# Moving sixteen modulation sums of VectorE from the stick-breaking attention to the retention, with attention steps 1.3 to a row

## The reference

```
mod = silu(c) @ w_ada + b_ada                 # 1024 -> 6144: shift1, scale1, gate1, shift2, scale2, gate2
hmix = rmsnorm(x) * (1 + scale1) + shift1
proj = hmix @ w_in                            # attention q, k, v; retention q, k, v, g; branch gates
o_sb  = stick_breaking_attention(16 heads of 64)
o_ret = silu(r_g) * head_rmsnorm(retention(rotary(q), rotary(k), v))   # 4 heads, q and k 256 wide, v 512
x = x + gate1 * ((g_sb * (o_sb @ w_proj_sb) + g_ret * (o_ret @ w_proj_ret)) @ w_out)
x = x + gate2 * ffn(rmsnorm(x) * (1 + scale2) + shift2)
```

## Time and profile before

| | |
|---|---|
| median of 3 runs | 2096.8 us (2093.87 to 2098.34) |
| the profiled execution | 2099.07 us, its span 2097.2 us |
| mean granted TensorE clock | 0.965 |
| attention with q, k, v and gate | about 61 to 330 us of the span |
| product with w_proj_sb | about 350 to 395 us |
| retention | about 395 to 850 us |

### The profile page before, as it was taken

The page is one execution under the profiler, slowest core; times in us unless marked ns, Lnnn a source line. Parts: engine busy times, 40 slices in busy tenths (PEclk is TensorE's granted clock), DMA queues, the critical chain, the costliest instruction groups (busy, mean ns, idle before and its releaser), DMA issues.

```text
span 2097.2 us, 21914 instructions
## 1 busy us (share of the span) xinstructions
PE 1955.8 (93%) x8805; PEld 1524.1 (73%) x8805; DVE 893.5 (43%) x1486; ACT 716.1 (34%) x1032; POOL 499.7 (24%) x270
## 2 busy tenths in 40 slices
PE   7989989999999999969599999998898889999998
PEld 6666667877777777857488888865775578888886
DVE  6677776203031313342133333468535554433433
ACT  5645464123332323332122223423236432222223
POOL 4322224444444434400000000132235411000000
PEclk9999999999999999979799999998998989999999
DMA  9323324421313123212522322421121122322321
GB/s 305 118 81 101 101 75 155 162 81 61 101 61 101 61 81 120 82 59 46 126 83 81 118 91 65 111 81 60 50 72 61 41 71 81 100 101 81 101 91 50
DMA packets 183771, 192.21 MB, mean 92 GB/s; under 512 B 10034, under 2 KB 167000, under 8 KB 183544
## 3 DMA queue, kind: packets, MB, share of 16 engines
q1 hardware_dynamic: 181816, 183.46, 27.6%
q10 hardware_dynamic: 1424, 5.00, 0.7%
q0 software_dynamic: 432, 2.36, 0.3%
HBM read 186.09 MB, written 4.72 MB: 91 GB/s over the span
## 4 chain that ended last, share of the span: by engine, by line
PE 45%; DVE 6%; DMA 2%; issue 2%; ACT 1%; POOL 0%; SPq 0%; DVEq 0%; ACTq 0%; POOLq 0%
PE bank L1402 12%; PE bank L1403 11%; PE bank L1405 11%; DMA stg<-in_w_ffn_in 2%; PE bank L1424 2%; PE bank L1423 2%; PE bank L1422 2%; DVE SW L2019 1%; DVE small L2017 1%; PE bank L1640 1%; PE bank L1662 1%; PE bank L1577 0%; DVE wl L1715 0%; PE bank L1528 0%; PE bank L1432 0%
## 5 line engine op out<-in xcount | busy, mean ns | idle before, releaser
L2541 POOL TENSOR_TENSOR wl<-stg,wh 128x1024 fp32r<-128x1024 f32 x150 | 362.1, 2415 | 1065.5 <-ACT wh L2199 1065.4
L1402 PE MATMUL bank<-hH,wh 128*128 128x512 f32 x1296 | 543.6, 419 | 47.6 <-DVE wl L1715 39.9
L1403 PE MATMUL bank<-hL,wh 128*128 128x512 f32 x1296 | 522.1, 403 | 0.0
L1405 PE MATMUL bank<-hH,wl 128*128 128x512 f32 x1296 | 521.4, 402 | 0.0
L2199 ACT ACTIVATE wh<-stg 128x1024 fp32r<-128x1024 f32 (+2 forms) x292 | 298.3, 1023 | 327.5 <-PE bank L1405 211.8
L1402 PEld LDWEIGHTS bank<-hH,wh 128*128 128x128 f32 x1296 | 249.8, 193 | 134.3 <-issue 79.0
L1405 PEld LDWEIGHTS bank<-hH,wl 128*128 128x128 f32 x1296 | 249.5, 192 | 61.0
L1403 PEld LDWEIGHTS bank<-hL,wh 128*128 128x128 f32 x1296 | 250.6, 193 | 51.7 <-issue 0.7
L1715 DVE TENSOR_TENSOR wl<-stg,wh 128x1024 fp32r<-128x1024 f32 (+2 forms) x142 | 168.4, 1188 | 270.1 <-ACT wh L2199 269.5
L1402 PE MATMUL bank<-h2H,wh 128*128 128x512 f32 x352 | 141.3, 402 | 0.0
L1405 PE MATMUL bank<-h2H,wl 128*128 128x512 f32 x352 | 140.7, 400 | 0.0
(11 more groups left out here) (321 smaller groups left out, 2763.2 us busy)
## 6 DMA issues: line engine op xcount, KB each, us to landing
stg<-in_w_in SPq DMA_DIRECT2D x54, 1024.0 KB, 5.1
stg<-in_w_ffn_in SPq DMA_DIRECT2D x22, 1024.0 KB, 5.1
stg<-in_w_ada SPq DMA_DIRECT2D x16, 1024.0 KB, 5.3
stg<-in_w_ffn_gate SPq DMA_DIRECT2D x11, 1024.0 KB, 5.1
stg<-in_w_ffn_up SPq DMA_DIRECT2D x11, 1024.0 KB, 5.1
stg<-in_w_ffn_down SPq DMA_DIRECT2D x10, 1024.0 KB, 5.0
stg<-in_w_ada SPq DMA_DIRECT2D x16, 512.0 KB, 6.5
stg<-in_w_proj_ret SPq DMA_DIRECT2D x8, 1024.0 KB, 4.9
```

Source lines behind the costliest of these rows:

```text
L1402: T.matmul(ps, wh, xh, start=j["first"] and k == 0, stop=False)
L1403: T.matmul(ps, wh, xl, start=False, stop=False)
L1405: t = T.matmul(ps, wl, xh, start=False, stop=j["stop"] and last)
L2541: G.tensor_tensor(lo, src, hi, ALU.subtract).then_inc(s["w_lo_pool"], 1)
```

## The change

The sixteen blocks leave the attention, the branch gate and the w_proj_sb product. One is placed behind every pair of jobs of q, k, v and g in the retention until all are used: six at head 0, six at head 1, four at head 2. `adasum` is no longer put off: it stands directly behind the pair of jobs, and takes its bank from "G" and no longer from "O". The sum lies in one buffer of its own, ADA, of 128x256, and a block's first DVE instruction waits for the `adasum` of the block before (it was two before). The attention's rate goes from 1 to 1.3 in the q, k, v jobs and in the branch gate's.

```diff
         def fn(n):
             for _ in p.jobs[n]["steps"]:
                 pass
-
-            def sums():
-                take("O", ("mod", a), 0)
-                emit("adasum", a)
-                give(("mod", a))
-            p.later.append([0, sums])
+            take("G", ("mod", a), 0)
+            emit("adasum", a)
+            give(("mod", a))
         return fn
...
-    left = list(range(8, 24))
     for p2 in range(1, 4):
         for kind, b0 in (("sbq", 0), ("sbk", 1024), ("sbv", 2048)):
             both(b0 + p2 * 256, kind, [(2 * p2,), (2 * p2 + 1,)], "w_in", "h1", after=v_after if kind == "sbv" else None)
-            ada(left.pop(0))
-        stage(1)
+        stage(1.3)
...
         both(O_BR + f2 * 256, "gate_sb", [(2 * f2,), (2 * f2 + 1,)], "w_in", "h1", after=tables_again)
-        if left:
-            ada(left.pop(0))
-    stage(1.0)
+    stage(1.3)
     do(p.finish)
     for f2 in range(4):
         both(f2 * 256, "proj_sb", [(2 * f2,), (2 * f2 + 1,)], "w_proj_sb", "os")
-        if left:
-            ada(left.pop(0))
     stage()
...
+    left = list(range(8, 24))
+
+    def more_ada():
+        if left:
+            ada(left.pop(0))
+
     def qk_jobs(hh):
         for what, o0 in (("q", O_RQ), ("k", O_RK)):
             b = p.block("w_in", o0 + hh * 256)
             for half in range(2):
                 p.job(b, half, rot_job(what, hh, half), x="h1")
+            more_ada()
...
(the same line at the end of each turn of the loops in v_jobs and g_jobs)
...
+        ADA = sb("ADA", [P, 256])
...
-            return TMP[7][:, 256 * (n % 2):256 * (n % 2) + 256]
+            return TMP[7][:, 256 * (n % 2):256 * (n % 2) + 256] if n < 8 else ADA[:, :]
...
-                        ve.wait_ge("pe_ada", n - 1)
+                        ve.wait_ge("pe_ada", n - 1 if n < 8 else n)
```

## The result

The changed kernel takes 2110.9 us (median of 4 runs, 2106.6 to 2111.5); the kernel before took 2096.6 beside it (4 runs, 2093.9 to 2098.3). The ratio is 1.0055, 95% interval 1.0039 to 1.0071: slower, clear of the noise, and 2.6 us from the forecast of 2108.3. The profiled execution is the fastest of the four, 2106.57 us with a span of 2104.8; that of before, 2099.07 us, lies above its four. The two profiled executions therefore differ by 7.5 us where the medians differ by 14.3; no trace tells where the other runs spent their 4 us more.

The account below looks back on a forecast made before the run. PE was taken to bound the retention alone, DVE to cost only in the attention. Terms: -2.7 - 1.7 - 1.4 + 1.5 + 10.7 + 5.1 = +11.5 us, giving 2110.6 profiled, 2108.3 as median; range 2086 to 2119.

Parts of the forecast that it names:

- Which stage is bound by what: DVE work costs something in the attention only; the retention is bound by PE alone, so waits there are paid in full.
- The bank: Retention: `adasum` takes a "G" bank, so PE waits 1.8 us for the rotation's third instruction, six times: +10.7 us.
- The clock: Stalls bring the lower granted clock, 1.7 us lost each: -1.7 us in the attention, +5.1 us in the retention.
- one less, -1.7 us: Attention: of six stretches at the lower clock one goes, -1.7 us (-8.5 to +1.7).
- Modulation out of the attention: Attention: removal saves 3.8 us a pair, rate 1.3 takes 2.1 back; waits become 17 us, -2.7 us (-13.6 to +5).
- The bare chain: Attention: at rate 1.3 PE stands 1.2 us in every pair from the attention's own DVE chain, without modulation.
- Cover and load: Attention, a pair: rate 1.3 costs 2.1 us of time PE covers for DVE; removed modulation instructions free 3.8 us.
- the rival by which the port hands its waits over: Attention: chain DVE instructions wait for the shared port instead; pairs +5 us, clock unchanged, 2117.7 us; chance 0.15.
- The start: Attention's start: up to one more softplus piece stands ahead of ACT's copy of q, +1.5 us.
- Bank 7: Attention: PE's wait at `adasum` behind the single bank 7 goes, -1.4 us.
- DVE's sums done 5 us before PE asks: Retention: DVE has room and finishes a block's sums some 5 us before PE asks; taken as 0 us (0 to +3).
- 16 us lower without it: Retention: were `adasum` left in bank 7, there would be no rotation wait and the sum would be 16 us lower.

Follow-up runs that it names:

- e1: The changed kernel with the bank of `adasum` taken from the two of "Z" instead of the three of "G": 2104.3 us, ratio to the kernel before 1.0023.
- e4: The changed kernel with the second and third instruction of the rotation (L1811, L1812) exchanged: 2107.7 us, ratio to the kernel before 1.0046.
- e11: e10 with the bank of `adasum` taken from "G", as in the change: 2100.4 us, ratio to the kernel before 1.0021.
- e3: The changed kernel with both attention rates back at 1, modulation still in the retention, `adasum` on "G": 2102.3 us, ratio to the kernel before 1.0021.
- e2: The kernel before with both attention rates at 1.3, the modulation left where it was: 2109.7 us, ratio to the kernel before 1.0054.
- e5: e1 with both attention rates back at 1: 2100.1 us, ratio to the kernel before 1.0014.
- e9: e1 with the retention's q, k, v and g jobs prepared three jobs ahead instead of two while modulation blocks are left: 2104.5 us, ratio to before 1.0037.
- e10: e9 with the attention's rates at 1: 2095.8 us, ratio to the kernel before 0.9992.
- e12: e10 with `adasum` put off by one job and two halves of a sum buffer: 2088.1 us, ratio to the kernel before 0.9961.
- e14: e12 with the attention's rates at 1.3: 2092.5 us, ratio to the kernel before 0.9982.
- e15: e12 with the attention's rates at 0.9: 2072.8 us, ratio to the kernel before 0.9887.
- e13: e12 with two jobs of lead instead of three: 2095.8 us, ratio to the kernel before 0.9998.

## Why the prediction was right

- *Which stage is bound by what*: right. The retention paid for its waits in full.
- *The bank*: right, and shown by e1, e4 and e11. 12.7 us in six waits against 10.7; 10.2 of it are the wait as reckoned, six times 1.70 us against 1.8, and the rest is DVE late twice, which I had named without a price. No run has the bank of "G" with `adasum` put off, so what the bank costs by itself there stays open.
- *The clock*: the retention's 6.8 us against 5.1. In the attention the step "one less, -1.7 us" was wrong in size: five of six stretches went, 8.5 us. The stalls before were up to 2.6 us; in the changed kernel none at L1464 is over 1.82. But stalls of 1.82 us were followed by a stretch before, and the one of 1.82 in the changed kernel isn't, so why five went stays open.
- *Modulation out of the attention*: 3.6 us at the cumulative sums against 2.7, 2.0 us a pair against 2.1. The bare chain came as reckoned: of the seven waits for L1778, five are 1.1 to 1.4 us, against 1.2. The balance is right by luck in part: e3 and e2 show 6.9 us given by the modulation and 3.7 taken by the rate, where I had 3.8 and 2.1 us a pair, 30 and 17. Cover and load were priced as if each microsecond of them counted in each pair. The lengthened instructions I had taken as constant: in the changed kernel the CAST is never lengthened, L1778 is instead, from a mean of 693 before to 865 ns, and L1772 has 802 against 824 before:

```profile
L1778 DVE TENSOR_TENSOR spl<-tmp,sph 128x512 fp32r<-128x512 f32 x37 | 32.0, 865 | 1.3
L1772 DVE SCALAR_TENSOR_TENSOR tmp<-zs,tmp 128x512 f32<-128x512 f32 x37 | 29.7, 802 | 0.0
...
L1776 DVE CAST sph<-tmp 128x512 fp32r<-128x512 f32 x37 | 15.8, 427 | 1.3
```

  Over the 685 of an undisturbed L1772 and the 693 of L1778 that is 4.3 + 6.4 = 10.7 us, against 15.4. So the rival by which the port hands its waits over falls in the changed kernel, -3.6 us in place of +5. In e3, at rate 1, it is borne out in part: the chain's lengthening rises to 20.8 us, though PE's waits fall all the same. The rule behind it, that an instruction with two SBUF inputs can be held up too (the Trainium skill, SBUF — State Buffer, Who interferes with whom), agrees with L1778, which had shown none of it before and now takes 2.82 us once beside GpSimd:

```profile
137.64 2.39 POOL L2542 TENSOR_TENSOR wl<-stg,wh 128x1024 fp32r<-128x1024 f32 x1 [10.96 <-ACT wh L2200]
137.75 2.82 DVE L1778 TENSOR_TENSOR spl<-tmp,sph 128x512 fp32r<-128x512 f32 x1
```

- *The start*: 1.8 us against 1.5. *Bank 7*: 1.4 us gone, as said; two further waits, 2.25 us for the last exponential and 0.35 us at the scores, went too and stood in no term.
- *DVE's sums done 5 us before PE asks*: held in the changed kernel, where PE was late itself. e5, e9 and e10 show waits of 5.6, 4.2 and 3.7 us at the longest once the bank is repaired. The rule of rotating banks (the Trainium skill, Perfetto Trace Analysis, Optimizing Tensor Performance) holds, but "16 us lower without it" did not: e1, with the banks of "Z", gave 6.6; bank 7 itself was not tried in the retention.

The mechanism that decides, the bank, was right; the nearness of the number was luck. Up to the retention I had -4.3 us, and the traces show -14.3; in the retention +15.8, and they show +19.3; for what lies behind and the rest nothing, and they show +2.5. So the profiled executions differ by 7.5 us against the 11.5 forecast, and the medians by 14.3, on the other side; this spread stays open.

## What to carry to other kernels

Work moved beside an engine that is never idle must not touch that engine's queue: look at its bank order, at what preparation is counted in jobs and at who issues what before whom, not only at the time that the mover's engine has free. When one wait is repaired and the time doesn't move, read the trace again before dropping the idea: here bank, lead and deferral each hid the next, and only all three together (e12, e14, e15) brought the time clear of the noise below the kernel before. In a stage where PE covers for a chain on another engine, fewer steps a row is cover; try the rate downwards as well. Set such a counter back between stages, or a change in one stage reorders the ones behind it and its price can't be read from the total.

## What was not expected of the hardware

- The granted clock pays more than the waits do: from the kernel before to the changed one the waits before the first rotation fall by 5.7 us, and the time at 0.50 from 20.5 to 3.4 us, which gives back 8.5. The length of a stall doesn't tell what follows: the 4.2 us wait at the start went with 3.4 us at 0.50 in the changed kernel and with 6.8 in e1, and a 1.70 us wait in the retention with 6.8.
- A stage that is left alone moves by several microseconds. Seven kernels (before, e3, e5, e10, e11, e12, e13) have the same work in the same order behind the retention, and up to the last feed-forward network they take 878.7 (e10) to 886.7 us (e11), one trace each; the time at 0.50 in it is 97.1 against 113.3 us, and half of that difference is all of the 8.0. What sets it off isn't shown.
